# Products of constant tiles on TensorE ahead of nine of its waits, in a two-block transformer kernel

## The reference

```
first block, layer:   h = rmsnorm(x)*(1+sc1)+sh1 ; u = h @ w_in          (1024 -> 5632)
                      pooling, short convolution, 8-head attention on u, gated and merged
                      x += g1 * (merged @ w_out)
                      h2 = rmsnorm(x)*(1+sc2)+sh2
                      x += g2 * ((silu(h2 @ w_gate) * (h2 @ w_up)) @ w_down)      (width 2816)
second block:         h = layer_norm(x), then per layer:
                      proj = h @ w_in_2 ; 8 MLA heads, 4 differential heads, 4 forgetting heads
                      h = layer_norm(ALPHA*h + o @ w_out_2)
                      scores = sigmoid(h @ router_w) ; one group of 4 experts, the best 2 in it
                      h = layer_norm(ALPHA*h + sum_e gate_e * expert_e(h))        (16 experts)
```

## Time and profile before

| | |
|---|---|
| median of three runs | 2061.66 us (2057.35 to 2066.27) |
| profiled execution | 2065.25 us, span 2063.6 us |
| mean granted TensorE clock | 0.914 |
| PE busy | 1731.6 us, 84% of the span |
| DVE busy | 977.6 us, 47% |
| ACT busy | 618.5 us, 30% |
| HBM traffic | 207 GB/s over the span |

### The profile page before, as it was taken

The page is one execution under the profiler, slowest core; times in us unless marked ns, Lnnn a source line. Parts: engine busy times, 40 slices in busy tenths (PEclk is TensorE's granted clock), DMA queues, the critical chain, the costliest instruction groups (busy, mean ns, idle before and its releaser), DMA issues.

```text
span 2063.6 us, 24382 instructions
## 1 busy us (share of the span) xinstructions
PE 1731.6 (84%) x8558; PEld 1233.6 (60%) x8558; DVE 977.6 (47%) x1442; ACT 618.5 (30%) x874; POOL 28.3 (1%) x57
## 2 busy tenths in 40 slices
PE   2789778889498977899887878999978786999996
PEld 1567657778376855778666665444437665544442
DVE  6776567543575657744465742111125574111112
ACT  2334433332334444343243710111113461011111
POOL 2000000000000000000010000000000000000000
PEclk9999989999798988999987978999998797899998
DMA  8774347644485434545464035999965303599994
GB/s 302 263 247 143 123 163 250 219 160 160 152 287 201 143 104 155 173 151 173 141 173 135 1 122 177 371 370 370 371 233 159 123 1 122 208 371 370 370 370 161
DMA packets 199017, 427.69 MB, mean 207 GB/s; under 512 B 8048, under 2 KB 16416, under 8 KB 198912
## 3 DMA queue, kind: packets, MB, share of 16 engines
q1 hardware_dynamic: 195328, 417.43, 58.0%
q0 software_dynamic: 3328, 8.86, 1.6%
q10 hardware_dynamic: 256, 0.08, 0.0%
HBM read 425.29 MB, written 1.05 MB: 207 GB/s over the span
## 4 chain that ended last, share of the span: by engine, by line
PE 52%; DVE 6%; issue 3%; ACT 1%; DMA 1%; DVEq 0%; POOL 0%; ACTq 0%; SPq 0%
PE gp L2191 16%; PE gp L1851 10%; PE gp L2017 8%; PE gp L2177 6%; PE mp L2132 4%; PE mp L2075 1%; PE mp L2085 1%; PE mp L2086 1%; PE mp L2036 1%; PE gp L2149 1%; PE mp L2094 1%; PE gp L2210 1%; PE gp L2208 1%; DVE acc L1048 0%; PE mp L2107 0%
## 5 line engine op out<-in xcount | busy, mean ns | idle before, releaser
L1114 DVE TENSOR_TENSOR wlo<-raw,whi 128x2048 fp32r<-128x2048 f32 (+1 forms) x132 | 289.7, 2195 | 285.8 <-ACT whi L722 282.9
L1851 PE MATMUL gp<-whi,xt_hi 128*128 128x512 f32 (+1 forms) x800 | 321.2, 401 | 63.8 <-DVE xt_lo L1158 32.1
L722 ACT ACTIVATE whi<-raw 128x2048 fp32r<-128x2048 f32 (+1 forms) x132 | 242.0, 1835 | 399.3 <-PE gp L1851 290.1
L1851 PE MATMUL gp<-wlo,xt_hi 128*128 128x512 f32 (+1 forms) x800 | 314.0, 393 | 0.0
L1851 PE MATMUL gp<-whi,xt_lo 128*128 128x512 f32 (+1 forms) x800 | 313.6, 392 | 0.0
L2191 PE MATMUL gp<-raw,pr 128*64 128x512 f32 x768 | 233.2, 598 | 0.0
L2191 PE MATMUL gp<-raw_more,pr 128*64 128x512 f32 x768 | 227.4, 594 | 4.2 <-DVE pr L1732 2.4
L1851 PEld LDWEIGHTS gp<-whi,xt_hi 128*128 128x128 f32 x800 | 156.3, 195 | 107.0 <-issue 43.8
L1851 PEld LDWEIGHTS gp<-whi,xt_lo 128*128 128x128 f32 x800 | 156.0, 195 | 31.8
L1851 PEld LDWEIGHTS gp<-wlo,xt_hi 128*128 128x128 f32 x800 | 156.3, 195 | 29.8 <-issue 0.5
L2177 PEld LDWEIGHTS gp<-pr,x 128*128 128x128 f32 x1088 | 130.5, 200 | 31.3 <-issue 26.0
(11 more groups left out here) (360 smaller groups left out, 2261.2 us busy)
## 6 DMA issues: line engine op xcount, KB each, us to landing
raw<-in_w_in SPq DMA_DIRECT2D x60, 1024.0 KB, 5.6
raw<-in_w_ada SPq DMA_DIRECT2D x48, 1024.0 KB, 5.4
raw<-in_exp_w_gate SPq DMA_DIRECT2D x34, 1024.0 KB, 6.3
raw_more<-in_exp_w_down SPq DMA_DIRECT2D x34, 1024.0 KB, 7.2
raw<-in_exp_w_up SPq DMA_DIRECT2D x32, 1024.0 KB, 8.5
raw_more<-in_exp_w_up SPq DMA_DIRECT2D x32, 1024.0 KB, 9.3
raw_more<-in_exp_w_gate SPq DMA_DIRECT2D x30, 1024.0 KB, 7.1
raw<-in_exp_w_down SPq DMA_DIRECT2D x30, 1024.0 KB, 5.1
```

What stands on the lines that cost most here:

```text
L722: act.activation(slot(whi, s % SPLIT, units, cols), slot(raw, g % RAW, units, cols), ACT.Copy).then_inc(hi_done.sem, 1)
L1114: dve.tensor_tensor(slot(wlo, s % SPLIT, units, cols), slot(raw, g % RAW, units, cols), slot(whi, s % SPLIT, units, cols).bitcast(F32), AL ...
L1851: mm = pe.matmul(gp[:, q % 2, t, 0:wide], a[:, chunk, ts], w[:, unit, c0:c0 + wide], start=first and n == 0 and m == 0, stop=last and n == ...
```

## The change

A helper `keep_busy(bank, n)` issues n matmuls with the identity tile stationary and the 128x384 tile `mask` (the first attention's causal mask, 0 and -1e30) moving, both fp32 and both constant, into the first 384 columns of a PSUM bank. Each starts and stops its own sum, waits for nothing and signals nothing; nobody reads the result. It is called at eight places of PE's program, ahead of the waits listed above. The second block begins behind both the 28 at the loop's end and the 12 that stand between the loops.

```diff
--- before.py
+++ after.py
@@ -1826,6 +1826,11 @@
                 mm.then_inc(acc_read.sem, 1)
 
 
+            def keep_busy(bank, n):
+
+                for _ in range(n):
+                    pe.matmul(bank[:, 0:3 * P], ident[:, :], mask[:, :], start=True, stop=True)
+
             pe.wait_ge(params_ready, LAYERS)
             sum_mod(0, 0)
             sum_mod(1, 0)
@@ -1956,6 +1961,7 @@
                         pe.wait_ge(*ft_lo.at(l, X_MERGE + 2 * (s - S_OUT) + 2))
                     product(s)
 
+                keep_busy(mp[:, 3, :], 27)
                 pe.wait_ge(*xn_ready.at(l, 4))
                 for b in range(4):
                     turn(b, xn2, 2 * P * b).then_inc(tr_done.sem, 1)
@@ -1994,8 +2000,10 @@
                     if s == S_LAYER - 2:
                         pe.wait_ge(*ft_lo.at(l, X_LAYER))
                     product(s)
-
-
+                keep_busy(mp[:, 3, :], 28)
+
+
+            keep_busy(mp[:, 3, :], 12)
             with pe.Fori(0, LAYERS) as l:
                 def low_ready(n, turn):
 
@@ -2106,6 +2114,7 @@
                     pe.matmul(mp[:, 3, HD:2 * HD], pt2[:, P:2 * P], v[:, 0, :], start=True, stop=False)
                     pe.matmul(mp[:, 3, HD:2 * HD], pt2[:, 2 * P:3 * P], v[:, 1, :], start=False, stop=True).then_inc(o2_done.sem, 1)
 
+                keep_busy(mp[:, 1, :], 18)
                 for i in range(AJ + 4):
                     if 0 <= i - 1 < AJ:
                         scores(i - 1)
@@ -2116,6 +2125,7 @@
                     if 0 <= i - 3 < AJ:
                         turn_p(i - 3)
 
+                keep_busy(mp[:, 1, :], 12)
                 pe.wait_ge(*oa_ready.at2(l, 1))
                 for b in range(4):
                     turn(b, oa, 2 * P * b).then_inc(tr_done.sem, 1)
@@ -2134,6 +2144,7 @@
 
                 uses = [2 * sum(1 for q in range(J2_MOE) if q % 2 == p) for p in range(2)]
 
+                keep_busy(mp[:, 3, :], 24)
                 pe.wait_ge(*h_ready.at2(l, 2))
                 for b in range(4):
                     turn(b, x, 2 * P * b).then_inc(tr_done.sem, 1)
@@ -2149,6 +2160,7 @@
                             mm = pe.matmul(small[:, 2 * NE * t:2 * NE * (t + 1)], a[:, c, ts], rw2[:, c, :, :].rearrange("p a n -> p (a n)"),
                                            start=c == 0 and m == 0, stop=c == KD - 1 and m == 1)
                 mm.then_inc(logits_done.sem, 1)
+                keep_busy(mp[:, 3, :], 10)
 
                 pe.wait_ge(*chosen.at2(l, 1))
                 picked = rank[:, :, :].rearrange("p (t g) i -> p t (g i)", t=NT)
@@ -2245,6 +2257,7 @@
                     down(S2_LAYER - 2, 0)
                     add_result(NE)
                     scatter(last=True).then_inc(y_done.sem, 1)
+                    keep_busy(bank_tr, 30)
 
                     pe.sem_inc(w_used.sem, 6 * NE)
                     pe.sem_inc(tr_done.sem, 2 * NE)
```

## The result

The changed kernel takes 2091.6 us (median of 4 runs, 2083.44 to 2103.22); the kernel before, run beside it on the same chip, 2060.89 (4 runs, 2057.35 to 2066.27). The ratio is 1.0151, interval 1.009 to 1.0212: slower by some 31 us, where 23.2 were forecast. The profiled execution took 2085.4 us, near the lower end of its runs, against 2065.25 for the one of before, so the traces show only 20 us of the 31. 2091.6 lies 6.6 above the predicted 2085 and inside the range.

What follows compares the result with a forecast made beforehand. PE, busy 84% with idle waits at norms and the router's choice, was taken as the bound; 9.6 + 0 + 4.2 + 1.4 + 1.0 - 1.4 + 2.4 + 6 = 23.2 us slower, so 2085 us, range 2066 to 2098.

Steps and rivals of the forecast that it cites:

- Price: One added product of 384 columns: 0.64 us at full clock, bounds 0.64 and 1.29.
- Second norm: Added products overrun the 11.61 us wait; first product 5.1 late, 4.8 us counted per layer, 9.6 for two.
- Loop's turn, second block: Loop's turn: 0, as DVE reads later anyway; ahead of the second block: 5.6 late, 1.4 given back, 4.2 us.
- Attention: Calls before and after the attention: 0.7 and 0.5 us late, each twice, so 1.4 and 1.0 in the sum.
- Behind the experts: Late turns hidden behind DVE's two splits, nothing late; faster products behind give -1.4 us.
- Program's end: The last 30 added products run past the old end of the span: 2.4 us.
- Router: Router's norm to scatter: -4.9 us if the clock stays up, +6 if it falls; +3 taken per layer, 6 for two.
- 1 (clock stays up through the router): Rival: router gives -4.9 instead of +3 in each layer, time 2069 us; chance 15%.
- 2 and 3 (cheaper product): Rivals: product below 0.53 us, no turn late, about 2043, 7%; or so cheap that nothing changes, 2062, 2%.
- 4 (low clock everywhere, 2104): Rival: the low clock returns everywhere, all bounds at their upper ends, 42 us added, 2104 us; chance 5%.
- The rule that the prediction set against the change (27): Transposes do not count as busy, so the clock falls behind calls followed by turns: 27 us instead of 23.

Runs made afterwards that it cites:

- e4: Kernel before plus only the 27 added products (384 columns) ahead of the second norm's turns; 2071.04 us, ratio 1.0046.
- e8: Kernel before plus only the router's calls, 24 products ahead of its turns and 10 ahead of the choice, 384 columns; 2070.76 us, ratio 1.0034.
- e3: Kernel before plus only the 30 added products behind the experts; 2069.56 us, ratio 1.0036.
- e9: Kernel before plus only the attention's calls, 18 products ahead of it and 12 behind it, 384 columns; 2068.15 us, ratio 1.0023.
- e10: Kernel before plus only 28 products at the loop's end and 12 between the blocks, 384 columns; 2066.7 us, ratio 1.001.
- e2: The change with all eight calls and their counts kept, but 256 columns instead of 384; 2056.51 us, 0.9973 of the kernel before.
- e1: The change with all eight counts cut to fit their waits (18, 20, 6, 12, 9, 16, 8, 14); 2064.67 us, 1.001 of the kernel before.
- e7: Kernel before plus only 14 products of 384 columns at the top of the second block's loop body, behind the branch; 2063.48 us, ratio 1.0005.
- e5: The change with only the second norm, router and choice calls (27, 24, 10), at 256 columns; 2055.27 us, 0.9977 of the kernel before.

## Why the prediction came out as it did

**The parts add up to the change.** Each ratio less 1, times 2062 us:

| part | in the sum | measured (interval) |
|---|---|---|
| second norm (e4) | 9.6 | 9.5 (4.7 to 14.2) |
| router and choice (e8) | 6.0 | 7.0 (4.3 to 9.9) |
| behind the experts, middle and end (e3) | -1.4 + 2.4 = 1.0 | 7.4 (3.9 to 10.9) |
| attention, before and after (e9) | 1.4 + 1.0 = 2.4 | 4.7 (1.2 to 8.2) |
| loop's turn and second block (e10) | 0 + 4.2 | 2.1 (0.2 to 3.9) |
| sum | 23.2 | 30.7 (change: 31.1, interval 18.6 to 43.7) |

The sum of the parts has an interval of some 23 to 38, if their errors are independent, so that it is luck that 30.7 and 31.1 agree so closely.

The mechanism was right: 0.64 us a product, too many of them for every wait, a delay that passes on or is hidden according to who waits, and a clock that returns little. e2 shows it by the product's price alone, e1 by the counts. One term lies far outside the measured interval, the one behind the experts; it makes up 6.4 of the 7.9 us between the sum and the change. The last pair is 0.3 past its own.

**Price.** Right: 0.32 a half at full clock. Bounds 0.64 and 1.29 were both met, the upper one by the first products of a call that starts at the low clock; two calls paid in between, the choice (8.24 us for ten in the change, 0.41 a half, from the low clock as foreseen) and the call behind the attention, which I had priced at full clock. That assumption, that all calls but one follow dense work at full clock, failed there in the change's first layer: 10.2 us for twelve instead of 7.7. In its second layer it held, with 7.8.

**Second norm.** Right in all its steps: turns 17.25 behind the last product (17.1), first product 5.2 late (5.1), clock at 0.50 behind it, L1399 waits not shrunk: 27.7 us in twelve after, 28.0 before:

```profile
PE gp L1856 <- DVEq L1399: 27.7, 12, 5.1
```

**Loop's turn, second block.** Right in the trace to some tenths (+0.3; +5.6, then -1.4 with the clock at 1.00 in 1055.22 to 1058.30). The timed ratio of e10 puts the two at 2.1, and the traces of the change and of e10 both show 4.2 left at that point. Where the rest returns isn't shown.

**Attention.** Forecast 2.4, measured 4.7, within its interval. In the change's trace the turns before it came 3.2 late and nothing of that was left where the scores begin to flow (-0.5 in both layers, +0.7 forecast). The call behind it cost +3.4 in the first layer, at the price of the fallen clock, and +0.3 in the second, at the full one (+0.5 forecast). In e9's trace, of the slowest of its ten runs, the first call left +3.1 and +0.2, the clock having fallen once more for 10 us inside the first layer's scores, and the second +3.2 and +2.0. So the price was too small where the clock was low, and the size per layer depends on where it falls, which a single trace doesn't settle.

**Behind the experts.** This step failed. "Turns at 1553.6 give ACT the bank at 1554.3, and DVE has it at 1555.0: nothing late" reckons only with data. PE's sequencer, which issues its products, has two branches to take between the experts' last scatter and the turns: the one that ends the `If` around the experts, and the one back to the loop's head. Their rows (count, then durations in ns as smallest, median, largest, and first and last start), the second branch before, then both in the change:

```profile
L1999 PEldq COMPARE_BRANCH  x1: 4869/4869/4869, 1536.4 to 1536.4; - x1
...
L2269 PEldq COMPARE_BRANCH  x1: 4357/4357/4357, 1562.6 to 1562.6; - x1
L2007 PEldq COMPARE_BRANCH  x1: 4756/4756/4756, 1567.1 to 1567.1; - x1
```

Before, the second was over at 1541.3, 6 us ahead of the vector, and cost nothing. In the change the sequencer enters the first at 1562.6, while added products issued ahead of it still run to 1568.2, and leaves the second at 1571.9; the turns start at 1572.03. PE so stood 3.82 us in the change, 4.12 in e3 and 5.04 in e2, with nothing else that the profile shows to wait for. e7, with its products behind the jump, starts them at 1540.13, 0.2 behind the end of its second branch. At the turn of the first block's loop there is one branch only, 3.8 us from 547.8 in the change, and it ends under the 28 products, so that nothing shows.

Why a branch takes so long is less sure. The stretch holds fetches of instructions (the DMA queues: packets, MB, share of 16 engines, in 1565 to 1573 of the change):

```profile
q8 instruction: 2, 0.03, 2.6%
```

Before, the same 16 KB fetches stood at 1533.9 to 1538.0, inside the two branches. That they wait for the arrival of code is thus supported by the place, but no run changed the code's size alone. Ahead of the jump this wait of 12.8 us offers some 8 to 9 us, and 30 products fill 19.2; e1's 14 fill 9.0, and its turns come on time. The forecast -1.4 became +4.9 at the first product in the change's trace and +5.3 in e3's, and once the clock was up again, as the forecast counts it, +4.1 and +4.2. The return of 1.6 that stood in it is real where the turns are on time: 1.5 in e7's trace. Even the price that e2 pays does not save this place: its gap of 5.04 made the product 1.1 late, given back behind it.

**Program's end.** Right: the last added product ends at 2083.49, the span at 2083.7; +2.6 in the trace for 2.4. In the last layer the calls' 19 us serve no later work at all.

**Router.** Right by its size (+3.0 and +3.1 per layer in e8, +3 forecast), and in part by luck. +3 was a value that I had set between two branches that were worked out, -4.9 with the clock kept and +6 with it lost, and neither came as it stood. In e8 the logits start 3.35 late (3.65) and the small sums return 1.1 (1.1), but logits and choice together cost 1.0 and 2.6 where the lost clock had 3.5, since in the first layer the clock fell only towards the end of the logits, and in the second layer the gather took 5.2 instead of 7.09. In the change itself it took 5.79 and 5.7, a return that I had put at nothing; the scatter hardly moved (3.24 for 3.47). In the change's own trace the net was +1.7 and -0.1; the timed ratio of e8 supports the larger size.

**The rivals.** 1 (clock stays up through the router): from the router's turns to the experts the clock averages 0.77 in the change, 0.73 in e8 and 0.71 in e5, and the gather, which would take 3.8, took 5.2 to 7.1 in all of them. Out as a whole, though in the change's second layer the logits themselves ran at 1.00. 2 and 3 (cheaper product): out by the pitch; that all would turn at a lower price is nevertheless right, e2 being faster than before at 0.43 a product, with gains of 5 us where the rival had 19. 4 (low clock everywhere, 2104): not as a whole, but its 0.5 behind the experts was still below what was measured. The rule that the prediction set against the change (27) comes nearer to 31 than its sum, but not for its reason: returns that the rule strikes out did come, 1.4 ahead of the second block and 1.5 behind the experts in e7.

## What to carry to other kernels

A filler instruction is a delay with a known price: count how many fit between the last work and the release of the wait, at the price that the engine's state there gives, and round down; past that point each goes in full to whoever waits (27 products for 17.3 us in a wait of 11.6 cost 5 us a layer, 27 at two thirds of the width gained half a microsecond). Ahead of a jump, part of the wait is already taken by the branches themselves (two of 3.4 and 4.9 us before, here). What a warm clock gives back is little (some 0.5 us at a norm whose consumer idles on, 3.5 us a layer in a chain of small products), so such a filling is worth it only where the slow stretch behind it is long, and it must be renewed there.

## What the runs showed of the hardware

- A busy PE can lose the clock. Products of 32 columns kept PE busy 100% of 20.19 us at a granted clock of 0.57 (2.4 GHz falling to 1.2, the halves 0.11 us apart and then 0.213), where the calls at the same norm with 256 and 384 columns kept 1.00.
- Turns alone brought the clock back. In the kernel before, PE did nothing for 11.61 us ahead of the second norm's turns and then nothing but turns, and the clock rose among them (columns as in the stretches above; the clock is 0.50, then 1.00):

```profile
304.73:307.45 2.72, 2.72 (x13) 2.72 (x14) 1.44 (x3) 0.32 (x1) 0.00 (x0) 0.50 0.00 0
307.45:308.00 0.55, 0.55 (x5) 0.31 (x3) 0.51 (x2) 0.31 (x1) 0.00 (x0) 1.00 0.00 0
```

The Trainium skill says that transposes do not count as busy for the clock ("TensorE: Matmul & The Clock Gate", section Part 4: PE-mode transpose). These rows speak against it, as the prediction had it.

- After a fill at 1.00, turns of 1.91 us ran at 1.00, and the products behind another 3.56 us of idling ran at 0.50 (315.89 to 319.48), those behind 0.87 us of idling at 1.00 (1055.22 to 1058.30). This pair doesn't tell whether turns count, since PE was off other products for 5.5 us in the one case and 2.8 in the other, turns included.
- PE's sequencer spends 4.6 to 5.1 us in the branch back to the head of the second block's loop, in the kernel before as in the others, and 3.4 to 4.4 us in the one just ahead of it. Work already issued runs on meanwhile; PE stands idle for the rest, 3.8 to 6.7 us in the change, e2, e3 and e7, and in the kernel before the norm's wait covers it.
- The mean clock is a poor measure of gain: 0.962 in the slowest of these kernels, 0.93 in the fastest, 0.914 before.
- Not settled: why e1 gains nothing while e2 gains 5.6 us. The eight products of 384 columns that e1 has at the choice start at the low clock and overrun the wait, and the router gains 0.9 and 1.0 us instead of 3.4 and 3.6, which is 5.0 of the 8; the rest isn't traced.
